# Two-layer trunk with product-key experts: the expert search ordered by drains, three row signals told less often, one key block kept on chip

## What is computed

```
q = (xn @ w_query)                          # 8 heads, two halves of 128
s = einsum(q, subkeys)                      # per head and half: 128 scores a token
s1, i1 = top_k(s[first half], 16);  s2, i2 = top_k(s[second half], 16)
top_s, top_c = top_k(s1[:, None] + s2[None, :], 16)      # of 256 sums
idx  = i1[top_c // 16] * 128 + i2[top_c % 16]            # 16 of 16384 experts
gate = softmax(top_s)
act  = gelu(u_tbl[idx] . xn)
out  = sum over heads and k of gate * act * v_tbl[idx]
```

## Time and profile before

| | us |
|---|---|
| runs: median of 3 | 1704.74 |
| lowest, highest | 1693.55, 1705.69 |
| profiled execution, its own time | 1688.29 |
| span of the profiled execution | 1686.3 |
| mean granted TensorE clock | 0.879 |

### The profile page before, as it was taken

How to read it: one execution, slowest core, us unless ns; L and a number is a source line. 1 busy time by engine, 2 the same in 40 slices (tenths; PEclk the granted TensorE clock), 3 DMA queues, 4 the chain that set the end, 5 groups by cost and what they waited for, 6 DMA issues and landing times.

```text
span 1686.3 us, 15100 instructions
## 1 busy us (share of the span) xinstructions
PE 1325.6 (79%) x4882; PEld 765.0 (45%) x4882; DVE 1052.9 (62%) x2495; ACT 366.5 (22%) x843; POOL 988.3 (59%) x1038
## 2 busy tenths in 40 slices
PE   9989788778768798849876899878987786665556
PEld 8976544344335454324543455535454442222222
DVE  3447477656766576655767845566667663866665
ACT  1111232112212223222212232133222221211101
POOL 0046466667666566646566765466666656666754
PEclk9989899889789898868898999889997988777778
DMA  9589999999999999999999999799999989899997
GB/s 333 178 302 339 359 340 358 375 391 382 381 368 355 342 401 406 399 408 404 385 404 378 360 400 404 293 397 328 373 406 365 349 299 385 323 365 368 377 334 301
DMA packets 197713, 607.66 MB, mean 360 GB/s; under 512 B 17597, under 2 KB 50437, under 8 KB 197637
## 3 DMA queue, kind: packets, MB, share of 16 engines
q0 software_dynamic: 147456, 536.94, 83.4%
q1 hardware_dynamic: 50048, 69.73, 11.9%
q10 hardware_dynamic: 132, 0.04, 0.0%
HBM read 605.59 MB, written 1.05 MB: 360 GB/s over the span
## 4 chain that ended last, share of the span: by engine, by line
PE 39%; DVE 16%; issue 14%; DMA 10%; POOL 10%; another core or an unknown queue 7%; ACT 3%; SPq 1%; POOLq 0%; DVEq 0%; ACTq 0%
PE sums L897 24%; POOL rows L654 10%; DVE rows L1707 8%; PE banks L754 8%; DMA rows<-in_peer_u,expert 6%; PE banks L771 4%; DMA rows<-in_peer_v,expert 3%; DVE h L1698 1%; DMA wring<-in_attn_w_q 1%; PE banks L780 1%; PE sums L763 1%; DMA h<-in_x 1%; DVE find L1606 1%; ACT soft_diag L1274 1%
## 5 line engine op out<-in xcount | busy, mean ns | idle before, releaser
L897 PE MATMUL sums<-rows,soft_diag 128*128 128x512 f32 x1764 | 865.4, 648 | 255.5 <-ACT soft_diag L1274 127.4
L654 POOL DMA_INDIRECT rows<-in_peer_v,expert x512 | 502.4, 981 | 448.8 <-PE sums L897 190.1
L1707 DVE SCALAR_TENSOR_TENSOR rows<-rows,xn_near 128x1024 f32<-128x1024 f32 x512 | 603.3, 1217 | 206.6 <-DMA rows<-in_peer_u,expert 176.6
L897 PEld LDWEIGHTS sums<-rows,soft_diag 128*128 128x128 f32 x1764 | 361.8, 209 | 727.7 <-issue 587.7
L654 POOL DMA_INDIRECT rows<-in_peer_u,expert x512 | 483.8, 945 | 235.8 <-issue 147.8
L1274 ACT ACTIVATE soft_diag<-ident,coef 128x128 f32<-128x128 f32 x446 | 138.4, 389 | 39.7 <-issue 22.6
L1266 ACT ACTIVATE gelu<-dots 128x8 f32<-128x8 f32 (+1 forms) x65 | 13.5, 208 | 582.7 <-DVE rows L1707 341.1
L1698 DVE SCALAR_TENSOR_TENSOR h<-rows,coef,h 128x1024 f32<-128x1024 f32 x63 | 80.7, 1281 | 0.0
L754 PE MATMUL banks<-xT,wring 128*128 128x128 f32 x512 | 65.0, 285 | 13.0 <-issue 10.6
L754 PEld LDWEIGHTS banks<-xT,wring 128*128 128x128 f32 x512 | 63.0, 201 | 18.0 <-issue 17.8
L1769 DVE SCALAR_TENSOR_TENSOR soft_diag<-banks,soft_diag 128x512 f32<-128x512 f32 (+1 forms) x8 | 7.7, 958 | 98.0 <-ACT soft_diag L1299 66.5
(11 more groups left out here) (209 smaller groups left out, 1019.7 us busy)
## 6 DMA issues: line engine op xcount, KB each, us to landing
wring<-in_w_kv SPq DMA_DIRECT2D x14, 1024.0 KB
rows<-in_peer_u,expert POOLq DMA_INDIRECT x512
rows<-in_peer_v,expert POOLq DMA_INDIRECT x512
wkept<-in_peer_w_query SPq DMA_DIRECT2D x8, 1024.0 KB
rows<-in_conv_w_in SPq DMA_DIRECT2D x7, 1024.0 KB, 11.9
wring<-in_peer_w_query SPq DMA_DIRECT2D x7, 1024.0 KB
wring<-in_attn_w_q SPq DMA_DIRECT2D x7, 1024.0 KB
wkept<-in_conv_w_out SPq DMA_DIRECT2D x4, 1024.0 KB
```

The costliest lines, as they stand in the source:

```text
L654: nc.gpsimd.indirect_dma_start(row[j], None, table, bass.IndirectOffsetOnAxis(ap=expert[n % 2][:, k:k + 1], axis=0)).then_inc(landed[j], 16)
L897: last = nc.tensor.matmul(sums[:, half, :], diag[:, k % GROUP, :], v_row[k % V_SLOTS][:, half * 512:(half + 1) * 512], start=(first and k ...
L1707: nc.vector.scalar_tensor_tensor(out=u_row[j], in0=u_row[j], scalar=1.0, in1=xn_near[:, :, :].rearrange("p a d -> p (a d)"), op0=ALU.mult, ...
```

## The change

1. In find_experts the scores are read where they are, without the copy. Both sides go side by side. No instruction in it increments dve_step or waits for it; where one needs an earlier result, a drain of DVE stands between. top_ready is told by the second maximum of the sums.
2. dot_done is told after dots 3 and 7 of a group, v_used after rows 1, 3, 5 and 6, diag_ready after diagonals 0 and 6: 8 times in place of 22. The waits ask for the count that covers their row.
3. The first key block is loaded once, in three DMAs, into parts of value and keyT that are free from the end of the convolution until the keys and values of the second chunk are written. Both chunks' first key projection reads it there. The two loads into slot 0 go. SP waits for out0 before it.

```diff
+    DOTS_BY = GROUP // 2
+    USED_AFTER = (1, 3, 5, 6)
+    DIAG_AFTER = (0, 6)
+    def dots_count(K, j):
+        return GROUP // DOTS_BY * K + j // DOTS_BY + 1
+    def used_count(K, row):
+        return len(USED_AFTER) * K + sum(r < row for r in USED_AFTER) + 1
+    def diag_count(K, row):
+        return len(DIAG_AFTER) * K + sum(r < row for r in DIAG_AFTER) + 1
...
-    stream_key(0, 0)
     stream_qry(0, 1)
...
-    stream_key(1, 0)
...
-    ALSO = {BLOCK["key", 0, 0]: FILL["query", 0, 1, 1], ...
+    ALSO = {BLOCK["values", 0, 0, 1]: FILL["query", 0, 1, 1], ...
...
+                if m == BLOCK["qry", 0, 0]:
+                    sp.wait_ge(bank_done, FILL["out0", 1] + 1)
+                    w_key = w_kv.rearrange("(k p) n -> p k n", p=P)
+                    sp.dma_start(value_half, w_key[:, 0:KT // 2, 0:COLS]).then_inc(key_landed, 16)
+                    for s in range(2):
+                        sp.dma_start(keyT_half[:, :, s, :], w_key[:, KT // 2:, s * P:(s + 1) * P]).then_inc(key_landed, 16)
...
-                    pool.wait_ge(dot_done, GROUP * (K - 1) + j + 1)
+                    pool.wait_ge(dot_done, dots_count(K - 1, j))
                     gather(u_row, j, u_table, n, g * GROUP + j, u_landed)
                 for j in range(GROUP):
                     if j < BY_PE:
-                        pool.wait_ge(v_used, BY_PE * (K - 1) + j + 1)
+                        pool.wait_ge(v_used, used_count(K - 1, j))
...
+            def key_to_features(c):
+                bank = take("key", c, 0)
+                pe.wait_ge(key_landed, 16 * 3)
+                for s in range(2):
+                    for k in range(KT):
+                        last = nc.tensor.matmul(bank[:, s * P:(s + 1) * P], kept_key(k, s), kvT[:, k, :],
+                                                start=(k == 0), stop=(k == KT - 1))
+                last.then_inc(bank_done, 1)
...
-                    pe.wait_ge(diag_ready, PE_ROWS * n + BY_PE * g + k % GROUP + 1)
+                    pe.wait_ge(diag_ready, diag_count(GROUPS * n + g, k % GROUP))
...
-                    last.then_inc(v_used, 1)
+                    if k % GROUP in USED_AFTER:
+                        last.then_inc(v_used, 1)
...
-                        act.wait_ge(v_used, PE_ROWS * n + BY_PE * (g - 1) + min(j, BY_PE - 1) + 1)
-                    nc.scalar.activation(diag[:, j, :], ident[:], ACT.Copy, scale=coef[b][:, k:k + 1]).then_inc(diag_ready, 1)
+                        act.wait_ge(v_used, used_count(GROUPS * n + g - 1, min(j, BY_PE - 1)))
+                    shaped = nc.scalar.activation(diag[:, j, :], ident[:], ACT.Copy, scale=coef[b][:, k:k + 1])
+                    if part is not None or j in DIAG_AFTER:
+                        shaped.then_inc(diag_ready, 1)
...
-                s = mark(nc.vector.tensor_copy(srch, src))
-                for p in range(2):
-                    e = top16(side_v[:, p, :], side_i[:, p, :], srch[:, p * KEYS:(p + 1) * KEYS],
-                              srch2[:, p * KEYS:(p + 1) * KEYS], s)
...
+                for values, _, all_keys, _ in sides:
+                    nc.vector.max(values[:, 0:8], all_keys)
+                nc.vector.drain()
+                for values, _, all_keys, rest in sides:
+                    nc.vector.match_replace(rest, values[:, 0:8], all_keys, FOUND)
+                for values, indices, all_keys, _ in sides:
+                    nc.vector.max_index(indices[:, 0:8], values[:, 0:8], all_keys)
+                nc.vector.drain()
+                for values, _, _, rest in sides:
+                    nc.vector.max(values[:, 8:16], rest)
+                nc.vector.drain()
+                for values, indices, _, rest in sides:
+                    nc.vector.max_index(indices[:, 8:16], values[:, 8:16], rest)
+                nc.vector.tensor_tensor(cand.rearrange("p (a b) -> p a b", b=TOPK), ...
+                nc.vector.drain()
+                nc.vector.max(top[b][:, 0:8], cand)
+                nc.vector.drain()
+                nc.vector.match_replace(cand2, top[b][:, 0:8], cand, FOUND)
+                nc.vector.tensor_scalar(negmax[:, b:b + 1], top[b][:, 0:1], -1.0, None, ALU.mult)
+                nc.vector.max_index(cand_i[:, 0:8], top[b][:, 0:8], cand)
+                nc.vector.drain()
+                nc.vector.max(top[b][:, 8:16], cand2).then_inc(top_ready, 1)
+                nc.vector.drain()
+                nc.vector.max_index(cand_i[:, 8:16], top[b][:, 8:16], cand2)
+                nc.vector.drain()
...
+                    if j % DOTS_BY == DOTS_BY - 1:
+                        dot.then_inc(dot_done, 1)
```

More of the change, by code:

```diff
@@ L372, in trunk @@
     HALVED = 2
[L373 removed]
+    ALSO = {BLOCK["values", 0, 0, 1]: FILL["query", 0, 1, 1], BLOCK["subkeys", 1]: FILL["values", 0, 1], BLOCK["qry", 1, 0]: FILL["heads", 0, 3],
             BLOCK["queries", 0, 3, 1]: FILL["qrys", 1]}
@@ L498, in trunk, with kept_key @@
         sums = ctx.enter_context(nc.psum_tensor("sums", [P, 2, 512], F32))
+        keyT_half = keyT[:, :, P:T].rearrange("p (k s) t -> p k s t", s=2)
+        value_half = value[:, 1, :].rearrange("p (k n) -> p k n", n=COLS)
+        def kept_key(k, s):
+            return value_half[:, k, s * P:(s + 1) * P] if k < KT // 2 else keyT_half[:, k - KT // 2, s, :]
         xn_near = ctx.enter_context(nc.psum_tensor("xn_near", [P, 2, 512], F32))
@@ L1002, in mixer_slot @@
                             score(0, *asked)
-                    to_features(take("key", c, 0), weights_of("key", c, 0), kvT, P)
+                    key_to_features(c)
                     to_features(take("qry", c, 0), weights_of("qry", c, 0), mixT, P)
@@ L1264, in weigh @@
                 ks = slice(g * GROUP + js.start, g * GROUP + js.stop)
-                act.wait_ge(dot_done, TOPK * n + ks.stop)
+                act.wait_ge(dot_done, dots_count(GROUPS * n + g, js.stop - 1))
                 nc.scalar.activation(gelu[b][:, ks], dots[b][:, ks], ACT.Gelu).then_inc(gelu_done, 1)
@@ L1675, in find_experts @@
-                need(d)
+                src = score_at(0, 1) if n == 1 else scores[:, at, :]
+                sides = [(side_v[:, p, :], side_i[:, p, :], src[:, p * KEYS:(p + 1) * KEYS], srch2[:, p * KEYS:(p + 1) * KEYS])
+                         for p in range(2)]
+                for values, _, all_keys, _ in sides:
[3 more added lines that the diff above has]
+                    nc.vector.match_replace(rest, values[:, 0:8], all_keys, FOUND)
@@ new lines, in find_experts @@
+                nc.vector.drain()
+                nc.vector.tensor_tensor(pick, pick, side_i[:].unsqueeze(2).to_broadcast([P, 2, TOPK, TOPK]), ALU.mult)
+                nc.vector.drain()
+                nc.vector.tensor_reduce(picked[:].rearrange("p a k -> p (a k)"), pick.rearrange("p a k j -> p (a k) j"), AX_X, ALU.add)
+                nc.vector.drain()
+                nc.vector.scalar_tensor_tensor(out=expert_f[:], in0=picked[:, 0, :], scalar=float(KEYS),
+                                               in1=picked[:, 1, :], op0=ALU.mult, op1=ALU.add)
@@ L1924, in _ @@
             for half, cols in enumerate(halves_of_d):
-                dve.wait_ge(v_used, PE_ROWS * last + BY_PE + len(TAIL_PE) + half)
+                dve.wait_ge(v_used, used_count(GROUPS * last, BY_PE - 1) + len(TAIL_PE) + half)
                 nc.vector.tensor_tensor(h[:, 1, cols], sums[:, half, :], h[:, 1, cols], ALU.add).then_inc(stream_ready, 1)
```

57 lines of the change are left out of this document (20 added, 37 removed).

## The result

| us | before | after |
|---|---|---|
| runs: median of 4 | 1700.26 | 1718.99 |
| lowest, highest | 1693.55, 1705.69 | 1708.31, 1723.74 |
| profiled execution, its own time | 1688.29 | 1708.31 |

Ratio 1.0116, interval 1.0074 to 1.0158: slower. I had forecast 1683, faster; the time lies inside the range and on the wrong side. The two profiled executions differ by 20.0 us, so the pair can stand for the runs (the medians differ by 18.7).

The account below looks back on a forecast made before the run. It took DMA transfers as the bound, running dry when late signals hold POOL. Search -24, diagonals +5 and key block -2.6 gave -22 us, on the median of 1704.74 forecasting 1683 us, range 1636 to 1722.

Parts of the forecast that it names:

- What a drain costs: DVE's search: a drain taken at its lower bound, 0.04 us; upper bound, held like an increment, gain gone.
- The search term: Expert search on DVE: removing stalls between its instructions gains 24 us, ends 0 and -61 us.
- How much of a stall reaches the end: DVE's searches: one half of two long stalls (15 of 29.7 us), a tenth of the other 93 us.
- Increments arrive late while the transfers are full: All engines: during full transfers signals come microseconds late, so POOL waits and the transfers run dry.
- the transfers are near their floor: Gathers: DMA nearly full, 607.66 MB at 409 GB/s being 1486 of 1686 us; only dry time can be won.
- Copies: Search on DVE: dropping 30 copies of 297 ns saves 8.9 us of DVE, counted at nothing beside its waiting.
- Used rows told in pairs: PE's row signals to POOL's v gathers: first gather waits for two rows, POOL catches up; no cost counted.
- rival 3: PE's row signals: pairs bring a second late signal of 2.29 us per group; slower, up to 1729 us; chance 0.14.
- Diagonals: ACT's signals to PE: second row waits for the seventh diagonal, 0.4 us in 12 groups; +5 us, ends 0 and +18.
- Key block: Key loads: two loads of 1.05 MB become one; -2.6 us, ends 0 and -5.
- rival 1: All engines' signals: lateness shrinks with fewer posts, cutting POOL's 278 us of waits; 1635 us; chance 0.15.
- Rival 2: Search and gathers: drains held like increments, or gather rhythm takes the gain back; -9 to +5 us, 1700 us; chance 0.31.

Follow-up runs that it names:

- e2: Kernel before with the key block kept on chip and the search by drains, signals told as before; 1705.52 us, ratio 1.0055 on chip 4.
- e4: The changed kernel (after), unchanged, run again on chip 4; 1716.27 us, ratio 1.0101 to the kernel before.
- e1: Kernel before with only the key block change, old search and signals told as before; 1700.55 us, ratio 1.0008 on chip 4.
- e3: The changed kernel with the old search by increments, keeping key block and fewer tells; 1699.32 us, ratio 1.0020 on chip 4.
- e6: e1 with four extra sums on DVE ahead of every search, to price a late search; 1568.54 us, ratio 1.0082 on chip 13.
- e14: Same kernel as e6, run on chip 12; 1566.49 us, ratio 1.0065 to the kernel before.
- e13: Same kernel as e5, run on chip 12; 1552.80 us, ratio 0.9982 to the kernel before.
- e9: The changed kernel (after), unchanged, run on chip 12; 1555.95 us, ratio 1.0000 to the kernel before.
- e18: The changed kernel with half of each v row gathered, run on chip 5; 1682.09 us in one run.
- e5: e1 with the search side by side without the copy, ordered by increments instead of drains; 1553.34 us, ratio 0.9986 on chip 13.
- e7: e1 with only v_used told less often, after rows 1, 3, 5 and 6; 1553.18 us, ratio 0.9985 on chip 13.
- e11: Same kernel as e2 (key block and drains, signals as before), run on chip 12; 1555.73 us, ratio 1.0000.
- e10: Same kernel as e5, run on chip 12; 1552.77 us, ratio 0.9982 to the kernel before.
- e17: Same kernel as e1 (key block alone), run on chip 5; 1689.12 us, ratio 0.9971 to the kernel before.
- e16: Same kernel as e5, run on chip 5; 1685.40 us, ratio 0.9954 to the kernel before.

## Why the prediction was wrong, step by step

**The step that failed: "What a drain costs ... I take the lower."** The reason that I gave, "the engine itself is not held; only the return of the count is", was an inference from increments that nobody waits for. The drains' own records show DVE held in them, with no count to post, for up to 5.4 us. The pauses of the search shown above grow with what lies ahead of the drain: 5.15 us behind eight recorded instructions, 2.34 behind two, 4.68 behind five, 1.67 behind one (1.19 behind five as the hold ended). So do the longest ones over all searches of after, e2 and e4: 1.67 us behind one, 3.0 behind two, 5.4 behind five, 5.2 behind eight. My reading is that the reports of finished instructions come late, one after another; an increment asks for those up to one result, a drain for all. It fits the four drained profiles of chips that hold; that it is the mechanism inside the engine is argued, not shown. The search term, in the sum at -24 us with ends 0 and -61, measured +8 us (e2 over e1) and +15 beside the fewer tells (e4 over e3). Its bounds had no end above zero, which they needed: I had set the upper one at "held like an increment", with no case for held longer. That the time fell inside the range all the same is no merit: its upper part stood there for other causes. The 123 us of stall in the sum were about 107, too: some 14 of them are the ordinary gaps under 0.1 us.

**How much of a stall reaches the end** ("one half", "a tenth" of the rest). e6 and e14 put it at 0.10 where nothing is held: 15 of 140 us, 13 by e14 over e13. Where signals are held no run priced it. In after, 58 us more of search came with 20 us; the drains' part is 49 us (e2 over e1) for 8, a sixth, and e1's 356 us is the lowest of four old searches there (356 to 402), so that this price is rough. The half was the size of the hole behind two searches; that the transfers partly make up for such a hole later is argued.

**Increments arrive late while the transfers are full.** The lateness is real where I saw it, but e9 shows that "full" doesn't bring it about (409 GB/s on chip 12, no hold), and e18 that it comes at a share of 0.73 too. It goes with the chip. So does **"the transfers are near their floor"**: nearer on 12 and 13, where after's span is 1555 us against the 1486 of 607 MB at 409 GB/s, than on the chip of the result, where before's lay 200 us over it.

**Copies**, counted at nothing: e5 has searches 0.7 us shorter than e7's on the same chip and the same time. Right, as far as the pairs in e7 cost nothing.

**Dots told twice**, +0: POOL's wait for them fell from 8 to 5 us, with one of 3.2 us as foreseen. Right.

**Used rows told in pairs.** In the sum +0, in rival 3 a second late signal in more groups. The traces show the rival's mechanism: waits at the third v gather were 14 us in 16 groups in before and 50 us in 32 groups in after; e3 has them too (49 us), e1 and e2 don't. Its price was too high: less was waited at the second, fourth and sixth gathers, and e3 takes 3 us more than e1, in an interval that covers -2 to +8. On chip 12 it is zero (e9 against e11). So rival 3 is right in what happens, wrong in what it costs alone; beside the drains the tells cost another 10 us (e4 over e2, 6 to 14), and why they cost more there no run shows. Slower was forecast at 0.14, for this cause alone.

**Diagonals**, +5: the distance from the start of PE's row 0 to that of row 1 is 3.38 us (median of 63 groups) with all diagonals told in e10, and 3.39 with two told in e9. I had row 0 at 1.75 us. It takes 3.4, and the rows behind it 1.75: at 1186.03 in e9 PE comes to it from a pause of 6.29 us, and over its 3.3 us the granted clock is 0.50 (1.2 GHz). So the seventh diagonal is told before row 0 ends. The term is 0 on chip 12, and no run takes it by itself where signals are held. **Key block**, -2.6 us: 0.9971 and 1.0008 in e17 and e1, so -4.9 and +1.4 us, each with an interval of 5 to either side; it agrees and isn't proved. On chips 12 and 13 no run has the key block alone; e5, e7 and e10, which have it, are 2.3 to 2.8 us faster than before. **Fewer posts shrink the waits** (rival 1): 278 us became 276, and by place the waits for PE grew by 4. Dead.

**What would show it**, as I had written: "searches still of 20 us (the drain is held)" is what came. Rival 2 began with that case, but priced it at nothing. Its remark that recording the trace isn't part of the stalls, since the profiled execution is no slower than the others, doesn't hold either: every run of this case comes with a span and a granted clock, so that, as far as these numbers tell, every run was recorded (see the last section).

The Trainium skill's "VectorE: DVE Perf Modes", section "The DRAIN you can't avoid", has increments cost nothing. Chips 12 and 13 agree: instructions follow one another by 0.04 us behind an increment and 0.07 behind a drain. Chips 4 and 5 don't, with pauses of up to 5.7 us behind an increment (e16) and 5.4 behind a drain.

## What to carry to other kernels

A drain is not a cheaper semaphore: it cost 8 to 15 us on chip 4, where completions are reported late, and 2.6 us on chip 12, where they aren't. Before pricing an unseen operation at its best case, ask what it waits for that the old one didn't, and let the ends of that term reach past zero. To learn what a delay is worth, add a known delay and divide; the holes in the transfers behind two long stalls overstated it three- to fivefold. And before believing a bound ("the transfers"), halve it: on chip 13 that moved the kernel by 86 us, on chip 5 by about 30.

## What was not expected of the hardware

- Two kinds of chip for one program: before takes 1693 to 1700 us on chips 4, 5 and the one of the result, and 1555 to 1556 on 12 and 13, with a spread of 27 us on chip 4 and 3.5 us on chip 13. The gap of 140 us goes with late signals: POOL idles 282 to 325 us there and 154 to 178 here with whole rows, and after's own kernel has 162 us less of it on chip 12 (e9), in a span 152 us shorter.
- On the first kind a DVE that only computes can stand for 5 us before its own next instruction, by an increment or by a drain alike. What holds the reports back is open. In after it comes only while transfers are at work: of its 31 searches the six whose first 9 us met less than 325 GB/s took 9.0 to 9.2 us, and of the other 25 only three took under 11. But e18's took up to 23 us with its first 9 us at 254 GB/s, so it is not the bytes alone.
- The traces differ by chip in one more way, which leaves a rival untested. On each of the 16 semaphores on which gathers land, the traces of chips 12 and 13 have 1,023 to 1,025 events; those of chips 4, 5 and the one of the result have 272 to 659 of these, and other semaphores lack events too. That would explain why so many waits there are put down to "issue" and "remote". The lateness may come of the recording itself, or late signals and lost events may have one other cause. Every run here comes with a span and a clock of its record; only a run without recording, on a chip of the first kind, could tell.
